# Feed-forwards of a two-block transformer kernel: plain three-pass products replaced by seven-product Strassen units

## What is computed

```python
def swiglu_ffn(h, w_in, w_out):
    gate, up = jnp.split(h @ w_in, 2, axis=-1)
    return (jax.nn.silu(gate) * up) @ w_out

x = x + swiglu_ffn(rms_norm(x, norm_ffn_g), w_ffn_in, w_ffn_out)            # first block: "fa"
x = x + 0.5 * swiglu(rms_norm_2(x, ffn1_norm), ffn1_gate, ffn1_up, ffn1_down)  # second block: "fb"
...
x = x + 0.5 * swiglu(rms_norm_2(x, ffn2_norm), ffn2_gate, ffn2_up, ffn2_down)  # second block: "fc"
```

## Time and profile before

| | |
|---|---|
| Median of 3 runs | 2423.3 us (2423.14 to 2424.0) |
| Profiled execution, first to last instruction | 2420.5 us |
| Beside the span, by the median | 2.8 us |
| PE busy (matmuls) | 2397.5 us, 99% |
| VectorE (DVE) busy | 1263.9 us, 52% |
| ScalarE (ACT) busy | 1002.5 us, 41% |
| GpSimd (POOL) busy | 331.9 us, 14% |
| The feed-forwards | fa from about 985 to 1345, fb from 1345 to 1706, fc from 2062 to 2411 us |

### The profile page before, as it was taken

One profiled execution on the slowest core, in us unless ns is written; L12 is line 12 of the kernel. 1 busy time (PEld: TensorE's weight loads), 2 busy tenths in 40 slices (PEclk: granted clock), 3 DMA queues, 4 the chain that ended last, 5 costly groups with the idle time before them and its releaser, 6 DMA issues.

```text
span 2420.5 us, 30412 instructions
## 1 busy us (share of the span) xinstructions
PE 2397.5 (99%) x12064; PEld 1956.4 (81%) x12064; DVE 1263.9 (52%) x1907; ACT 1002.5 (41%) x1634; POOL 331.9 (14%) x258
## 2 busy tenths in 40 slices
PE   8999999999999999999999999999999999999998
PEld 7777778777898888888888888888887888888887
DVE  5688746468765455443333544333678555333422
ACT  7766654234563344333223433222644454323321
POOL 0000000555100100111102111101032201101100
PEclk9999999999999999999999999999999999999999
DMA  6221235323665232332323332332322232333231
GB/s 203 71 70 51 86 99 183 113 68 108 200 210 209 96 105 70 105 95 88 96 97 101 99 97 90 96 100 88 111 63 63 87 113 74 101 96 105 97 100 56
DMA packets 172638, 251.65 MB, mean 104 GB/s; under 512 B 11472, under 2 KB 90576, under 8 KB 172496
## 3 DMA queue, kind: packets, MB, share of 16 engines
q1 hardware_dynamic: 171344, 248.13, 32.5%
q10 hardware_dynamic: 1152, 1.57, 0.2%
HBM read 231.83 MB, written 16.78 MB: 103 GB/s over the span
## 4 chain that ended last, share of the span: by engine, by line
PE 96%; DVE 2%; ACT 1%; issue 0%; POOL 0%; DMA 0%; DVEq 0%; SPq 0%; POOLq 0%
PE bank L1170 94%; PE bank L1299 1%; DVE wlo L2030 0%; PE bank L1322 0%; DVE T L2038 0%; PE bank L1447 0%; PE bank L1423 0%; DVE macc L2030 0%; PE bank L1265 0%; DMA raw<-in_w_in 0%; DVE xg L2034 0%; ACT whi L1541 0%; DVE ml L2038 0%; DVE bank L2336 0%; DVE W L2030 0%
## 5 line engine op out<-in xcount | busy, mean ns | idle before, releaser
L1170 PE MATMUL bank<-xh,whi 128*128 128x512 f32 x1784 | 710.1, 398 | 8.0 <-DVE wlo L2030 8.0
L1170 PE MATMUL bank<-xh,wlo 128*128 128x512 f32 x1784 | 696.6, 390 | 0.0
L1170 PE MATMUL bank<-xl,whi 128*128 128x512 f32 x1784 | 695.9, 390 | 0.0
L2030 DVE TENSOR_TENSOR wlo<-raw,whi 128x1024 fp32r<-128x1024 f32 (+2 forms) x406 | 500.2, 1234 | 337.2 <-ACT whi L1541 337.0
L1541 ACT ACTIVATE whi<-raw 128x1024 fp32r<-128x1024 f32 (+2 forms) x406 | 419.2, 1038 | 513.7 <-PE bank L1170 507.2
L1170 PEld LDWEIGHTS bank<-xh,whi 128*128 128x128 f32 x1784 | 335.7, 188 | 94.7 <-issue 20.2
L1170 PEld LDWEIGHTS bank<-xh,wlo 128*128 128x128 f32 x1784 | 335.4, 188 | 71.1
L1170 PEld LDWEIGHTS bank<-xl,whi 128*128 128x128 f32 x1784 | 336.0, 188 | 65.4
L2030 DVE TENSOR_TENSOR T<-bank,R 128x512 f32<-128x512 f32 x86 | 59.0, 687 | 344.3 <-PE bank L1170 344.3
L1170 PE MATMUL bank<-hh,whi 128*128 128x512 f32 (+1 forms) x536 | 206.9, 386 | 0.0
L1170 PE MATMUL bank<-hl,whi 128*128 128x512 f32 (+1 forms) x536 | 206.8, 386 | 0.0
(11 more groups left out here) (356 smaller groups left out, 3494.9 us busy)
## 6 DMA issues: line engine op xcount, KB each, us to landing
raw<-in_w_in SPq DMA_DIRECT2D x92, 512.0 KB, 3.6
raw<-in_w_ffn_in SPq DMA_DIRECT2D x88, 256.0 KB, 3.2
raw<-in_ffn_gate SPq DMA_DIRECT2D x88, 256.0 KB, 2.8
raw<-in_ffn_up SPq DMA_DIRECT2D x88, 256.0 KB, 3.1
raw<-in_ffn_down SPq DMA_DIRECT2D x44, 512.0 KB, 3.6
raw<-in_w_ffn_out SPq DMA_DIRECT2D x22, 512.0 KB, 3.6
raw<-in_w_xattn_kv SPq DMA_DIRECT2D x16, 512.0 KB, 4.4
raw<-in_w_kv_mem SPq DMA_DIRECT2D x16, 512.0 KB, 4.9
```

The source lines that it names most:

```text
L1170: return e.matmul(out, l, r, start=start, stop=stop, skip_group_check=skip)
L2030: return e.tensor_tensor(out, a, b, op)
```

## The change

The weights of a feed-forward are cut in units of 1024x256 (gate `G`, up `U`, index 0 to 10) or, on the way back, of 1024 rows in two thirds and 768 rows in the last by 256 columns (`D`, index 0 to 3, phases `ph` 0, 1, 2). In a unit the weight's 256-row pairs are the two rows of a 2x2 block matrix (`e` = 0, 1), its two 128-column halves the two columns; the activation's token halves (2x256) and its two feature chunks give the other matrix. Seven block products (`p` = 1 to 7) take the place of eight, in the form with 15 additions. Four additions on each weight unit run on GpSimd (`w_add`), four on the activation tile on VectorE for hidden features and for fb, on GpSimd for fa and fc (`op_sum`), and the results are put together from PSUM by ScalarE (`take`) and VectorE (`c11`, `c22`, `c21`, `c12`, `x_add`). One PSUM bank ("alpha") holds a running sum whose members are products 1, 6, 7 and 4 and is read after each of them; products 5 and 2, into other banks, lie between the second and the third. The first gate and up unit and the last phase of the way back stay plain (`whole`); there half of the matmuls' columns are issued as 2 x 256.

Every product is of 128x256 tokens. The loops now follow the order G0 U0 (plain), G1 U1 G2 U2 G3 U3, G4, D0 to D3, U4, G5 U5 ... G8, D0 to D3, U8, G9 U9 G10 U10, D0 to D3 (plain).

```diff
+        def units(tag, out, g, gc, u, uc, down, loc):
+            order = []
+            for ph, (first, last) in enumerate(((0, 4), (4, 8), (8, 11))):
+                for p in range(first, last):
+                    order += [("G", p, ph)] if p in (0,) or p not in (4, 8) else []
+                    order += [("U", p, ph)]
+                order += [("G", last, ph + 1)] if last < 11 else []
+                order += [("D", i, ph) for i in range(4)]
...
+                plain = ph == 2 if kind == "D" else i == 0
...
+                plan = [[], [(v2, add(1)), (v, hi("k2"))], [(v, lo("12")), (v2, add(3)), (v2, add(2)), (v3, LOAD[0])],
+                        [(v, hi("4")), (v, lo("k2")), (v2, add(4))], [(v, lo("4"))], [(v2, hi("k1")), (v3, LOAD[1])],
+                        [(v2, lo("k1")), (v2, hi("12"))], []]
...
+                order = [(1, u), (5, u), (6, u), (2, u), (7, u)] if plain else [(6, u), (5, u), (2, u), (7, u)]
+                order += [] if UN[v]["plain"] else [(1, v)]
+                order += [(4, u), (3, u)]
...
+                for kt in kts:
+                    key, k = operand_at(u, kt)
+                    w.wait_ge(*at("op lo", key, k, int(slot < 4)))
+                    r = operand_tiles(key, k)[1]
+                    begin, end = fresh and kt == 0, kt == x["nk"] - 1
+                    mm(out, a[:, kt, :], r[:, 7 + slot, :], begin, False, skip=not fresh)
+                    mm(out, a[:, kt, :], r[:, slot, :], False, False, skip=not fresh)
+                    ins = mm(out, c[:, kt, :], r[:, 7 + slot, :], False, end, skip=not fresh)
...
+            def w_add(u, i):
...
+                    ins = tt(s1, a21, a22, ALU.add)
+                elif i == 3:
+                    w.wait_ge(*at("w add", u, 1))
+                    ins = tt(a21, a21, a11, ALU.subtract)
+                elif i == 2:
+                    w.wait_ge(*at("w add", u, 1))
+                    ins = tt(s2, s1, a11, ALU.subtract)
+                else:
...
+                    ins = tt(s4, a12, s2, ALU.subtract)
...
+            def gate_r(u, block):
...
+                tt(t, t, R[:, c:c + 256], ALU.mult).then_inc(*up("ffn_gate", ("gate r", u, block)))
+
+            def gate_r2(u, j):
+                t = half_views(u)[j]
+                w.wait_ge(*at("gate silu", u, j))
+                tt(t, t, R[:], ALU.mult).then_inc(*up("ffn_gate", ("gate r2", u, j)))
...
+            def s_lo(u, g):
+                w.wait_ge(*at("s hi", u, g))
+                if not UN[u]["plain"]:
+                    w.wait_ge(*at("w add", u, 2 if g == "k1" else 4))
+                tt(raw_view(u, g, True), raw_view(u, g), hi_tile(u, g).bitcast(F32), ALU.subtract).then_inc(
+                    *up("w_lo", ("s lo", u, g)))
...
+            def c11(u):
+                n, b = side("gamma", u)
+                t = half_views(u)[0][:, 0:256]
+                w.wait_ge(*at("taken", u, 1))
+                w.wait_ge(*at("product", u, 2))
+                tt(t, b[:, 0:256], t, ALU.add).then_inc(*up("blocks", ("c11", u), ("side", "free", n)))
...
+            def take(u, p):
...
+                out = {1: t[0][:, 0:256], 6: t[0][:, 256:512], 7: t[1][:, 256:512]}[p]
+                w.wait_ge(*at("product", u, p))
+                copy(out, b[:, 0:256]).then_inc(*up("taken", ("taken", u, p)))
```

More of the change, by code:

```diff
@@ new lines, in build, with want, add, hi @@
+        wanted = set()
+        def want(u, what):
+            for kind, args in what if what is LOAD else (what,):
+                if u is None or (UN[u]["plain"] and (kind == "w_add" or args[0] in ("12", "4"))):
+                    continue
+                if (kind, u, args) not in wanted:
+                    wanted.add((kind, u, args))
+                    step(kind, u, *args)
+        def add(i):
+            return "w_add", (i,)
+        def hi(g):
+            return "s_hi", (g,)
+        def lo(g):
+            return "s_lo", (g,)
@@ new lines, in product @@
+        def product(u, p, kts=None, more=()):
+            nk = UN[u]["nk"]
+            kts = tuple(kts if kts is not None else range(nk))
+            for name, ring, among in {1: [("alpha", main, u % 2)], 2: [("gamma", side, u % 2)], 5: [("beta", main, 2 + u % 2)]}.get(p, ()):
+                if kts[0] == 0:
+                    ring.new(name, u, among=(among,))
+            step("product", u, p, kts)
+            pay()
+            if kts[-1] == nk - 1:
+                owed.append(lambda: finished(u, p))
+            point()
+            for x, what in more:
+                want(x, what)
@@ L1178, in weight_tile @@
                 out = b[:, 0:n] if g["nat"] else b[:, 0:g["ntok"]]
[L1179 removed]
+                last = i == g["ids"][-1]
                 w.wait_ge(*at("w lo", i))
@@ new lines, in s_hi @@
+            def s_hi(u, g):
+                x = UN[u]
+                if x["plain"]:
+                    w.wait_ge(*at("unit there", u))
+                else:
+                    w.wait_ge(*at("w add", u, {"k1": 3, "k2": 1, "12": 2, "4": 4}[g]))
+                if x["loc"] < 2:
+                    i = {("k1", 0): 0, ("12", 0): 1, ("k2", 0): 2, ("4", 0): 1, ("k2", 1): 2, ("12", 1): 3, ("4", 1): 3}.get((g, x["loc"]))
+                    if i is not None:
+                        w.wait_ge(*at("w used", x["base"] + i))
+                elif x["loc"] < 4 and g in ("12", "4"):
+                    w.wait_ge(*at("w used", x["base"] + 3))
+                if borrows(u):
+                    before = done(ago(u, 4 if g == "k1" else 3), 5, 6)
+                elif x["loc"] > 4 and g == "12" and UN[u - 2]["plain"]:
+                    before = done(u - 4, 1)
+                else:
+                    before = done(ago(u, 2), *OPS[g])
+                for event in before:
+                    w.wait_ge(*event)
+                src = raw_view(u, g)
+                copy(hi_tile(u, g), src).then_inc(*up("w_hi", ("s hi", u, g)))
```

804 lines of the change are left out of this document (620 added, 184 removed).

## The result

The changed kernel takes **2589.28 us** (median of 4 runs, 2587.12 to 2595.06) where the kernel before, in the same session, takes 2423.42: a ratio of 1.069, 95% interval 1.0675 to 1.0705. It is slower, as forecast, but by 166 us and not by 42, and it lies 59 us above the range. The profiled execution has a span of 2587.6 us.

A forecast was written before the change was run, and what follows sets the result against it. PE's matmul count bounded the old kernel; after the change, SBUF access shared by VectorE and GpSimd would stall PE in gate and up units. 2420.5 - 62.6 + 104 = 2462, 2465 with 2.8 us run offset; 8-in-10 range 2385 to 2530.

The forecast's parts named there:

- PE's count, -62.6 us: Matmuls of the three feed-forwards: 338.2 us each instead of 359.1, with 256-token matmuls 0.120 us apart; -62.6 us in all.
- VectorE and GpSimd exclude each other, instruction by instruction: Two-operand SBUF work of VectorE and GpSimd shares one resource; VectorE's work from a PSUM bank does not.
- Rival (a): The sharing does not bind or the lead is larger, so PE's count decides: 2361 us; chance 0.10.
- rival (b): GpSimd's additions take 1.04 us: 2411 us, 2378 without idleness; chance 0.22, together with a smaller demand.
- 24.7 us a pair, r = 13.0: Shared-access demand of a gate and an up unit, 12.36 us a unit; with 5% idle a unit really takes 13.0.
- each engine's sum is under 20.16: Gate and up pair: durations alone fit PE's 20.16 us, with GpSimd 15.1, VectorE about 17, ScalarE 13.
- The lead is won back in the four down units: Down units restore 6 us of free lag before each gate and up run, cutting each feed-forward's stall by 18 us.
- A down unit needs 8.4 and fits: A down unit's shared-access demand on VectorE and GpSimd is 8.4 us, within PE's time for a unit.
- The stall of 104 us: PE waiting in gate and up units at 5% idleness: 34.6 us a feed-forward, 104 in three.
- rival (c): In-order queues lock, PE waiting at product 4 behind ScalarE's read of product 7: 2519 us, up to 2553; chance 0.20.
- products 1, 6 or 2: Where a unit's PE pauses of 1 to 3 us would stand, put down to VectorE; product 4 or 7 would refute it.
- Other edits cost nothing that I can find: Other edits, such as x_scaled, loads and banks, add nothing; the last product's halves perhaps 1 us.

The follow-up runs named there:

- 4: Changed kernel with GpSimd's four weight additions per unit replaced by zero fills, results left out: 2407.02 us, ratio 0.9932 to the kernel before.
- 8: Changed kernel with each weight addition replaced by a chain of three fills as long as an addition, results left out: 2427.10 us, ratio 1.0015.
- 6: Changed kernel with the third and fourth weight additions of each unit replaced by fills, results left out: 2493.59 us, ratio 1.0288.
- 7: Changed kernel with weight additions moved to VectorE (first kernel), 2571.17 us; products with R moved too, GpSimd idle in a pair (second kernel), 2546.67 us.
- 2: Kernel of 1 with two more parts, one high and one low, placed behind the reads of product 7: 2566.55 us, ratio 1.0590.
- 3: Changed kernel with product 7 ahead of product 2 (order 6, 5, 7, 2): 2557.73 us, ratio 1.0552.
- 1: Changed kernel with the hidden sums' second high part and its low part one point later, behind ScalarE's read of product 7: 2576.16 us, ratio 1.0630.
- 5: Changed kernel with the second low part of a feed-forward's first unit asked for ahead of the unit behind it: 2581.8 us, ratio 1.0654.

## Why the prediction was wrong

- **PE's count, -62.6 us: right.** A Strassen unit takes 10.08 us wherever nothing waits, and the account closes with it. The shorter gap that the prediction quotes from the Trainium skill (TensorE: Matmul & The Clock Gate, Back-to-back issue gap), 109 ns at 256 columns, is not what these matmuls keep: 0.120 us.
- **VectorE and GpSimd exclude each other, instruction by instruction: right**, and shown to be the cause (4, 8). Rival (a), no binding, and rival (b), additions of 1.04 us, are out: a pair took 26.6 us, and of 336 additions the shortest took 1.28, their means being 1.6 to 1.8.
- **24.7 us a pair, r = 13.0: nearly right for a reason that was wrong.** The pair at 1197 us has r = 13.3, and so has the mean of six pairs (29.6, 25.0 and 27.2 us in the first run of the first feed-forward, 22.5, 28.3 and 26.6 in the second). The step "each engine's sum is under 20.16" counted VectorE as if only its two-operand work mattered. It left out 2.6 us from banks and the fixed part of short instructions; the 5% for idleness covered them by chance. The half dose (6) and the empty GpSimd (7) showed it.
- **"The lead is won back in the four down units", 6 us a run: the step that failed in the gate and up units.** At r = 13.0 without that credit of 18 us a feed-forward the stall is 158 us in three and not 104; measured are 168.5. A lead is there: the first pair behind four down units takes 22.5 us where later ones take 26.6. But each feed-forward starts without one, and its first Strassen unit alone runs 8 to 11 us over. By run, the three feed-forwards together, measured are 86, 69 and 13 us, where the forecast had 43, 52 and 8. On the whole nothing of the 54 us shows.
- **"A down unit needs 8.4 and fits": right of the work, wrong of the order.** Seen from the table's rule, with reads of banks, it needs 3 x 1.13 + 0.61 + 7 x 0.33 + 4 x 1.14 = 10.9, and it took 11.16 with a pause at product 4. But in 2 and 3, with all of that work, most down units take 10.08, so here the rule asks for too much. By order alone the 21 us that the down units cost fall to 13 and 11, and the forecast had no term for order. VectorE's timeline ahead of that pause, and PE's, in the changed kernel:

```profile
1130.22 1.98 DVE L2435 TENSOR_TENSOR wrawl<-wraw,wh 128x1024 fp32r<-128x1024 f32 x1
1132.12 0.41 DVE L2435 TENSOR_TENSOR xT<-xT,bank 128x256 f32<-128x256 f32 x1
...
1132.58 0.50 PE L1446 MATMUL bank<-hopr,wh 128*128 128x256 f32 x2 [0.82 <-DVE xT L2435]
```

- **The stall of 104 us: 190 in the same units.** The forecast's r is the real time of a unit, so what answers to it is waiting and half clock together; the 117.6 of waiting alone are near to 104 by chance. Its place was that of rival (c), product 4 behind ScalarE's read, and not products 1, 6 or 2, which I had named as a sign that the forecast is wrong. Taking (c)'s cause away (1 to 3) gave 13 to 32 us, so (c) is where the pause stands and not why it is there, and its own numbers, 2519 to 2553 us, were too low as well.
- **"Other edits cost nothing that I can find": wrong.** 40 us (waiting and half clock) stand at entries, ends and plain units, besides what the first Strassen unit of each feed-forward runs over. Two are the entries, 6.6 and 6.7 us (5). One is the last down phase of the first feed-forward, where a plain unit's low parts stand behind the sums of the next operand, 4.00 us beside GpSimd's sums of squares (timelines of VectorE and of PE in the changed kernel):

```profile
1372.40 4.00 DVE L2435 TENSOR_TENSOR xop<-xop 128x512 f32<-128x512 f32 x3
1376.33 1.48 DVE L2435 TENSOR_TENSOR xside<-xop,xside 128x256 fp32r<-128x256 f32 x1
1377.73 1.82 DVE L2435 TENSOR_TENSOR wrawl<-wraw,wh 128x768 fp32r<-128x768 f32 x2
...
1379.69 1.19 PE L1446 MATMUL bank<-hopr,wh 128*128 128x512 f32 x2 [6.55 <-DVE wrawl L2435]
```

- **No term for TensorE's clock: an omission, whose price stays open.** Before, PE never paused in a feed-forward, and every row had the full clock; that it would hold through pauses was assumed and not weighed. 63.0 us of the account are half clock, but they can't be put down as its price. Two pairs of units in a row, one at the full clock and one with 3.4 us at half, in the kernel of experiment 3 (first two lines) and in the first of experiment 7 (last two):

```profile
2337.79:2363.80 26.01, 21.27 (x171) 20.42 (x170) 23.23 (x25) 10.70 (x17) 21.12 (x14) 1.00 0.32 96
2363.80:2389.80 26.00, 22.46 (x171) 21.85 (x170) 23.22 (x25) 12.02 (x20) 21.11 (x14) 0.93 0.28 82
...
2211.42:2235.39 23.97, 20.66 (x169) 20.26 (x169) 23.38 (x33) 12.53 (x19) 8.60 (x5) 1.00 0.35 97
2235.39:2260.84 25.45, 22.16 (x168) 21.75 (x169) 23.60 (x33) 12.03 (x18) 7.97 (x5) 0.93 0.27 82
```

In 3 the slower matmuls cost nothing: a pair takes 26.0 us either way, and its pauses are shorter by the 1.4 us that its matmuls take more. In 7 they cost 1.5 us. In both pairs of 3 the longest pause is 2.3 us, so its length alone doesn't tell whether the clock falls. No run takes the half clock away from the changed kernel and nothing else.

The sum, by place: 2465 + 54 (no credit for the lead) + 11 (168.5 - 158) + 21 (down units) + 40 (entries and plain units) = 2591, against 2589.3. So the step that failed most is the credit, and then the entries with the plain units and the down units, both of which the forecast put at nothing. What stays open: how the 40 us divide among their places, beyond the entries and the few pauses that were followed, and which part of the half clock was a loss.

## What to carry to other kernels

Add up, for the engine that works in order, all of its own instructions at their distance from start to start, and on top every instruction of the engine that shuts it out; that sum, not either engine's busy share, is held against the matmuls. It is good to 1 or 2 us here: 22.0 by the sum where 23.05 were measured, but 28.1 where 26.6 were and 10.9 where 10.08 were, in units in which VectorE's reads of banks can lie beside GpSimd's work. An addition moved to an idle GpSimd costs VectorE 1.14 us here, and 0.61 if VectorE does it itself. A lead that is won in one stretch and spent in the next is worth checking at each place where it would have to exist, the entry above all. And where a forecast puts pauses of some us into a full TensorE, it has to ask whether the clock falls and whether TensorE is what sets the pace there: the same 3.4 us at half clock cost nothing in one kernel and 1.5 us in another.

## What the runs showed of the hardware

- Short instructions pay most for the exclusion: VectorE's product of 256 elements went from 0.42 to 1.07 us, since it waits for a whole operation of the other.
- A GpSimd fill of 512 elements takes 0.53 us and holds VectorE up by nothing that shows.
- Behind a pause of 3.9 us TensorE ran 6.2 us at a mean granted clock of 0.57, at first with 0.21 us a matmul of 256 columns; behind 0.82 us it kept 0.12.
